# DeltaNet stage of a three-block forward pass: order of the VectorE and ScalarE work between weight tiles

## The reference

```python
decay = jnp.exp(jnp.where(lower_incl, gc[..., :, None] - gc[..., None, :], -jnp.inf))
kb = k * beta[..., None]
lmat = jnp.where(strict, jnp.einsum('bhnid,bhnjd->bhnij', kb, k) * decay, 0.0)
tinv = lax.linalg.triangular_solve(eye + lmat, ..., left_side=True, lower=True)
u = tinv @ (v * beta[..., None])
w = tinv @ (kb * jnp.exp(gc)[..., None])
attn = jnp.einsum('bhnid,bhnjd->bhnij', q, k) * decay
k_dec = k * jnp.exp(g_last[..., None] - gc)[..., None]
# scan over 4 chunks of 64 tokens with a 128 x 128 state for each of 8 heads
v_new = u_i - w_i @ state
o_i = q_i @ state + attn_i @ v_new
state = state * jnp.exp(gl_i) + k_i.T @ v_new
# then
o = rms_norm_2(o, norm_w) * jax.nn.silu(z)
g_nsa, g_dn = jnp.split(jax.nn.sigmoid(merge_g), 2, axis=-1)
mixed = g_nsa * (o_nsa @ w_up_nsa) + g_dn * (o_dn @ w_up_dn)
```

## Time and profile before

| | before |
|---|---|
| median of three runs | 2406.88 us |
| profiled execution, its time | 2404.23 us |
| profiled execution, its span | 2402.5 us |
| mean granted TensorE clock | 0.991 |
| VectorE busy | 1468.0 us (61%) |
| ScalarE busy | 1296.1 us (54%) |
| GpSimd busy | 18.3 us (1%) |
| HBM over the span | 169 GB/s |

### The profile page before, as it was taken

How to read it: one execution, slowest core, us unless ns; L and a number is a source line. 1 busy time by engine, 2 the same in 40 slices (tenths; PEclk the granted TensorE clock), 3 DMA queues, 4 the chain that set the end, 5 groups by cost and what they waited for, 6 DMA issues and landing times.

```text
span 2402.5 us, 33358 instructions
## 1 busy us (share of the span) xinstructions
PE 2337.5 (97%) x12514; PEld 1985.3 (83%) x12514; DVE 1468.0 (61%) x2567; ACT 1296.1 (54%) x2393; POOL 18.3 (1%) x38
## 2 busy tenths in 40 slices
PE   8999999899999899999999999999999999999998
PEld 7877788788888899778787887888888888888887
DVE  4554565675665655886676566656666666665554
ACT  5645455665565544775555545555555555554444
POOL 1000000000000000000000000000000000000000
PEclk9999999999999999999999999999999999999999
DMA  6555566456435465656453225655666666665554
GB/s 213 158 167 149 165 203 194 139 158 183 124 123 192 142 184 165 186 158 197 143 166 118 83 80 176 220 185 180 186 188 189 186 191 185 188 205 190 191 190 167
DMA packets 247404, 408.94 MB, mean 170 GB/s; under 512 B 29713, under 2 KB 62529, under 8 KB 246865
## 3 DMA queue, kind: packets, MB, share of 16 engines
q1 hardware_dynamic: 243392, 393.20, 54.7%
q0 software_dynamic: 3136, 10.26, 1.2%
q10 hardware_dynamic: 720, 3.42, 0.4%
HBM read 400.53 MB, written 6.29 MB: 169 GB/s over the span
## 4 chain that ended last, share of the span: by engine, by line
PE 89%; DVE 5%; ACT 4%; issue 1%; DMA 0%; SPq 0%; DVEq 0%; ACTq 0%
PE banks L361 50%; PE banks L335 14%; PE banks L355 9%; PE banks L337 7%; DVE weights_low L306 2%; PE banks L644 1%; ACT weights_high L303 1%; PE banks L804 1%; PE banks L2221 1%; PE banks L2210 1%; PE banks L1681 1%; PE banks L815 0%; DMA weight_ring<-in_w_gla_in 0%; PE banks L1102 0%; PE banks L2283 0%
## 5 line engine op out<-in xcount | busy, mean ns | idle before, releaser
L306 DVE TENSOR_TENSOR weights_low<-weight_ring,weights_high 128x512 fp32r<-128x512 f32 (+3 forms) x1512 | 1007.1, 675 | 841.7 <-ACT weights_high L303 812.5
L303 ACT CAST weights_high<-weight_ring 128x512 fp32r<-128x512 f32 (+3 forms) x1512 | 910.2, 609 | 1002.8 <-PE banks L361 637.8
L361 PE MATMUL banks<-weights_high,hidden_T 128*128 128x512 f32 x3008 | 865.9, 400 | 10.8 <-DVE weights_low L306 9.6
L361 PEld LDWEIGHTS banks<-weights_high,hidden_T 128*128 128x128 f32 x3008 | 557.0, 189 | 135.3 <-issue 12.8
L361 PE MATMUL banks<-weights_low,hidden_T 128*128 128x512 f32 x1504 | 466.7, 391 | 0.0
L335 PE MATMUL banks<-hidden_T,weights_high 128*128 128x512 f32 x1408 | 385.1, 394 | 0.6 <-DVE residual L2829 0.6
L361 PEld LDWEIGHTS banks<-weights_low,hidden_T 128*128 128x128 f32 x1504 | 283.3, 188 | 61.6
L335 PEld LDWEIGHTS banks<-hidden_T,weights_high 128*128 128x128 f32 x1408 | 240.4, 189 | 32.9 <-DVE residual L2829 0.8
L337 PEld LDWEIGHTS banks<-hidden_T,weights_low 128*128 128x128 f32 x1408 | 216.5, 189 | 30.3
L337 PE MATMUL banks<-hidden_T,weights_low 128*128 128x256 f32 x1408 | 224.4, 281 | 0.0
L355 PE MATMUL banks<-hidden_T,weights_high 128*128 128x256 f32 (+3 forms) x1120 | 185.3, 286 | 6.9 <-DVE weights_low L306 5.9
(11 more groups left out here) (400 smaller groups left out, 1737.2 us busy)
## 6 DMA issues: line engine op xcount, KB each, us to landing
weight_ring<-in_w_in SPq DMA_DIRECT2D x168, 512.0 KB, 3.6
weight_ring<-in_w_gla_in SPq DMA_DIRECT2D x96, 512.0 KB, 3.8
weight_ring<-in_w_gate SPq DMA_DIRECT2D x88, 512.0 KB, 3.7
weight_ring<-in_w_ffn_up SPq DMA_DIRECT2D x88, 512.0 KB, 3.6
weight_ring<-in_w_down SPq DMA_DIRECT2D x88, 512.0 KB, 3.8
weight_ring<-in_w_mla_in SPq DMA_DIRECT2D x49, 512.0 KB, 3.6
weight_ring<-in_w_gla_out SPq DMA_DIRECT2D x32, 512.0 KB, 4.2
weight_ring<-in_w_mla_out SPq DMA_DIRECT2D x32, 512.0 KB, 4.3
```

Source lines behind the costliest of these rows:

```text
L303: nc.scalar.copy(hi, raw).then_inc(high_ready, 1)
L306: nc.vector.tensor_tensor(lo, raw, hi.bitcast(F32), ALU.subtract).then_inc(low_ready, 1)
L361: last = pe.matmul(ps[:, b + t, 0:width], a[:, t * P:(t + 1) * P], w, start=(k == 0 and n_th == 0), stop=(k == kt - 1 and n_th == 2))
```

## The change

Four edits, all of them in the order and the place of work of ScalarE and VectorE; TensorE's queue is the same but for the name of one semaphore.

- VectorE does one filler step instead of three ahead of the decay work of a pass, and (2, 6) instead of (1, 3) after its halves. The first corner of the system is taken there, and `b_lt` stands for it too.
- The block with the turned keys leaves VectorE. ScalarE copies the turned keys from PSUM into `d_kd` as they are, ahead of its scaling of the values, and signals `b_keys` after both. TensorE's turn of the corner waits for `b_keys` instead of `b_ct`.
- VectorE makes `d_kg` from `d_kd` in SBUF after levels 1 and 2 (a half in each) and scales `d_kd` in place by the decay left after level 5. Its fillers in levels 0 and 1 are (1, 2) and 2 instead of 1 each.
- After the second pass ScalarE has its two filler steps between the squares instead of ahead of them and one more behind, and the splits of the first four tiles of the up product stand between the last turns on both engines, instead of behind them and the fillers.

```diff
                 for hf in HALVES:
-                    pe.wait_ge(b_ct, 2 * bt + hf + 1)
+                    pe.wait_ge(b_keys, 2 * bt + hf + 1)
...
                     act.wait_ge(b_tok, 2 * bt + hf + 1)
+                    Sc(act.copy(part_of(d_kd, hf), bank(hf, 0)))
                     for j, m in enumerate(ms(hf)):
...
+                    act.sem_inc(b_keys, 1)
                     fill(2)
...
-                fill(2)
-            squares(bt, 1)
+                if bt + 1 < DN_H // HB:
+                    fill(2)
+            squares(bt, 2)
+            fill(1)
             next(turns)
             next(turns)
+            prod_up.split(act, 0, 0, 0)
             roots(bt)
-            next(turns)
-            next(turns)
-            fill(3)
-            prod_up.prime(act)
-            fill(1)
+            for k in range(1, 3):
+                next(turns)
+                prod_up.split(act, 0, 0, k)
+            prod_up.split(act, 0, 0, 3)
+            fill(4)
...
             for bt in range(DN_H // HB):
-                fill(3)
+                fill(1)
...
                     V(v.tensor_tensor(lt, bank(hf, 0), lt, ALU.mult))
+                    corner(0, hf)
                     v.sem_inc(b_lt, 1)
-                    fill((1, 3)[hf])
-                for hf in HALVES:
-                    v.wait_ge(b_tok, 2 * bt + hf + 1)
-                    V(v.tensor_tensor(by_head(d_kg, hf), bank_heads(hf, 0), col(d_bg, bt, hf), ALU.mult))
-                    V(v.tensor_tensor(by_head(d_kd, hf), bank_heads(hf, 0), col(d_eleft, bt, hf), ALU.mult))
-                    corner(0, hf)
-                    v.sem_inc(b_ct, 1)
-                    fill(2)
+                    fill((2, 6)[hf])
...
                     v.sem_inc(b_xd, 1)
-                    fill(1)
+                    fill((1, 2)[hf])
...
-                    fill(1)
+                    fill(2 if lv == 1 else 1)
                     if lv <= 2:
                         decayed_queries(bt, (2 * lv - 2, 2 * lv - 1))
+                        if lv == 1:
+                            v.wait_ge(b_keys, 2 * bt + 2)
+                        hf = lv - 1
+                        V(v.tensor_tensor(by_head(d_kg, hf), by_head(d_kd, hf), col(d_bg, bt, hf), ALU.mult))
...
+                for hf in HALVES:
+                    V(v.tensor_tensor(by_head(d_kd, hf), by_head(d_kd, hf), col(d_eleft, bt, hf), ALU.mult))
                 for ch in range(NCH):
...
             inverses(bt)
-            next(turns)
-            next(turns)
+            prod_up.split(v, 0, 0, 0)
+            for k in range(1, 3):
+                next(turns)
+                prod_up.split(v, 0, 0, k)
+            prod_up.split(v, 0, 0, 3)
             fill(4)
-            prod_up.prime(v)
             v.wait_ge(b_nrs, bt + 1)
```

More of the change, by code:

```diff
@@ L2122, in program @@
             "row_inputs", "rows", "row_exps", "decay_ready", "products", "systems_ready", "tokens"))
-        (b_ct, b_t1, b_t1c, b_x, b_xd) = (sem("dn_inv_" + n) for n in ("corner", "corner_times", "corner_times_copied", "update", "updated"))
+        (b_keys, b_t1, b_t1c, b_x, b_xd) = (sem("dn_inv_" + n) for n in ("tokens_copied", "corner_times", "corner_times_copied", "update", "updated"))
         (b_uw, b_uwc, b_sc, b_vn, b_sn, b_si, b_in, b_ind) = (sem("dn_" + n) for n in (
```

## The result

| | before | after |
|---|---|---|
| median of the runs made beside each other | 2406.85 us (4 runs, 2406.26 to 2407.22) | 2389.61 us (4 runs, 2387.57 to 2390.39) |
| profiled execution, its time and span | 2404.23, 2402.5 us | 2388.96, 2387.2 us |
| mean granted TensorE clock | 0.991 | 0.993 |
| TensorE busy | 2337.5 us | 2332.0 us |

The ratio is 0.9928 (95% interval 0.9914 to 0.9942): 17.2 us faster by the medians, 15.3 by the two profiled executions. In the code after, VectorE's L2471 to L2475 have become L2476 to L2480, the corner L2443, L2490 and L2491 are L2489 and L2490, ScalarE's new copy is L2367, its scaling L2370; the sigmoid is L2719, VectorE's multiply behind it L2727, and GpSimd's store and loads are L3003 and L3013.

The account below looks back on a forecast made before the run. TensorE, busy 97%, bounds the kernel; only its waits or half-clock time can be won. Savings 6.2 + 6.0 + 2.1 = 14.3 us take the profiled 2404.23 to 2389.9, or 2392.6 against the median 2406.88; range 2388.8 to 2400.0.

Parts of the forecast that it names:

- What bounds the kernel: Whole kernel: TensorE is busy 97% of the span, so only its waits or half-clock time can be won.
- Decay work sooner and keys copied out: First and second DeltaNet pass: earlier VectorE decay work and ScalarE's key copies shorten TensorE's waits, saving 6.2 and 6.0 us.
- The waits forecast as 0.6 and 1.2: First pass, TensorE: some 0.6 us before tile 10 and 1.2 us before the second level-1 product.
- In the levels nothing is lost: Both passes: waits hide VectorE's moved multiplies, costing nothing; without cover, 2.9 us a pass.
- The tail: Up product: 4.0 us gained before tile 4, 2.0 lost waiting for the gates' path through DRAM; worth 2.1.
- A second fall of the clock: Rival, chance 0.26: a new 2.0 us wait near 1487 lowers TensorE's clock, costing 1.6 us; 2394.2 us.
- The gate path does not bind: Rival, chance 0.11: the gates' path through DRAM does not delay TensorE, so the tail gives 4.0 us; 2390.7 us.
- ScalarE has over 1.2 us to spare for each half: Rival, chance 0.12: ScalarE finishes the keys over 2.2 us late, corner turns wait, half of 12.2 is lost; 2398.7 us.
- The change does what it says: Rival, chance 0.05, said it doesn't: decay work still waits for exps or products, waits move a few tiles; 2405 us.
- Six splits in a row: Rival, chance 0.04: VectorE's splits 10 to 15 delay level 0 to 1303 in both passes, 5.5 us slower; 2412.4 us.
- The range: Whole kernel: 2388.8 (tail whole, 1.9 more waits gone) to 2400.0 us (half the levels lost, a clock fall).

Follow-up runs that it names:

- the extra multiplies: The changed kernel with the multiply that makes d_kg made three times in levels 1 and 2; 2393.74 us, ratio 0.9945.
- the kernel with the loads in another order: The changed kernel with GpSimd's gate loads issued in the order round 1, round 0, 2, 3; 2396.30 us, ratio 0.9958.
- levels alone: The changed kernel with its last part undone, so the tail is that of the kernel before; 2392.30 us, ratio 0.9942.
- decay sooner alone: The kernel before with only the order of VectorE's splits changed, one ahead of the decay work instead of three; 2397.10 us, ratio 0.9963.
- the decay late: The changed kernel with the decay work back behind three splits; 2398.70 us, ratio 0.9969.

## Why the prediction was right, and where it was off

The median lies 3.0 us under the forecast and inside the range, near its lower end.

- **What bounds the kernel**: right. Only TensorE's waits and its lower clock moved the time. VectorE's busy time fell by 0.3 us, ScalarE's rose by 2.2.
- **Decay work sooner and keys copied out** (6.2 and 6.0): measured 6.16 and 5.93. The start of tile 16 was forecast as 1303.3 and came at 1303.86 in an execution whose DeltaNet began 0.55 later; tile 44 at 1397.0 less 6.2 of the first pass is 1390.8, and it came at 1391.21. The waits forecast as 0.6 and 1.2 were 0.42 and 1.06. The experiments add what the sum could not: the first edit alone brings 5.3 and 4.2, and the second alone 1.6 and 1.6.
- **In the levels nothing is lost**: right, no wait stands there after. For level 2 of the second pass the text had a cover of 0.05 us left; the extra multiplies show 0.1, by far the tightest of the four places.
- **The tail** (2.1): the term that was mis-sized. It measured 3.6. The first part was right, 4.07 for 4.0. Taken back were 0.40 and 0.06, not 2.0. The step that failed is the length of the second gate load, taken over as 7.5 from the earlier trace rows; it measured 5.6. Measured from the DeltaNet's start and with the passes' 12.2 taken off, the store is issued 2.0 sooner (forecast 1.9), GpSimd's wait for it is 0.3 longer (6.35 against 6.03), and the load is 1.9 shorter. So the sigmoid begins 3.6 sooner where 1.9 was forecast. The mechanism was right for the new kernel: the sigmoid of after starts with the landing, and in the kernel with the loads in another order each microsecond of it is one of TensorE. In before itself the landing was not what decided, or not alone: the table load ended at 1486.04, last by less than 0.1 us. I took one load, issued 0.26 us behind a weight load, as the length in the new kernel. In after that neighbour was issued 2.27 us ahead; whether this is why the load was shorter stays open.
- **A number that agrees by luck.** Put on top of the levels, the tail's edit is worth 2.1 in the table (217.4 against 215.3), as forecast. But it is 2.5 gained before up tile 4 and 0.4 taken back, not 4.0 and 2.0, because in levels alone the clock had stayed up without it.
- Beside this: the Trainium skill, DMA: Bandwidth & Descriptors, section on the anatomy of a DMA on the gpsimd path, gives an estimate of 3.2 us for this load. The traces do not agree: the second gate load took 5.4 to 7.5 us. The 4.0 that this page would have left in the tail was nearer to the result than my 2.1, though its length was not.
- **The rest of the miss**: of 17.2 us, 15.8 lie in the stretch of the table, 1.5 more than the sum. The other 1.4 lie outside it, between profiled executions and medians, and say nothing of the mechanism. Before's profiled execution was 2.65 under its median, and the forecast added these 2.65 again; after's was 0.65 under its own, with its DeltaNet 0.55 later. Against the profiled execution the forecast was 2389.9, and 2388.96 came.
- **The rivals.** A second fall of the clock did not come, as the new wait was 0.22, not 2.0; with 2.97 it does. "The gate path does not bind" gave the nearer time (2390.7). Its conclusion was wrong, as the path binds in after, but its reasons were partly right, and I dismissed them too easily. The second gate load was shorter in the new kernel, and the table load had ended at 1486.04 in before. The landing at 1486.0, which I held against it, could not decide between the two. ScalarE has over 1.2 us to spare for each half. The change does what it says. Six splits in a row end at 1292.52 + 0.69, 2.7 us before the turned corner is there; split 15 was placed at 1292.5.
- **The range**: its upper end adds up to 2400.3 by its own terms (2392.6, 6.1 and 1.6), not 2400.0; this changes nothing.

## What to carry to other kernels

Where one engine's queue feeds TensorE both weight splits and the links of a dependent chain, what is needed later goes behind what is needed sooner: putting the chain's first operations two splits forward brought most of the passes' gain, with no work removed. A wait found behind the one that was taken away should be worked out in the time frame of the new kernel. A DMA in it is a range from several rows of the trace with different neighbours, not one row. And a difference of one or two microseconds in 2400 is read from the traces, between the same instructions, since the medians carry falls of the clock from stretches that were not touched.

## What the runs showed of the hardware

- **The same wait with and without a fall of the clock.** After a wait of 2.22 us ahead of up tile 0 the granted clock fell to 0.50 (1.2 GHz) in before and in decay sooner alone, and stayed at 1.00 (2.4 GHz) in levels alone, with the same tiles ahead of it. Waits of 1.34 and 1.73 us in a row were followed by the lower level in before, 0.55 and 1.73 in decay sooner alone were not. Waits of 2.62, 2.64 and 2.97 were. So a fall cannot be told from the length of the last wait alone; what else decides, these runs leave open. I had expected the limit to lie between 1.92 and 2.22.
- **Its price** was 1.6 us each time it could be taken alone: 18.09 against 19.66 to up tile 4, and 10.97 against 12.58 to up tile 20. In the first pass of before it was more: from the second level-1 product to tile 16 it took 5.14 us (1304.33 to 1309.47), in after 2.80.
- **Loads of the same 512 KB** on GpSimd's queue, the first of a row of four issued 0.5 us apart, took 3.9 to 5.9 us, the second 5.4 to 7.5, the fourth up to 9.6. With SyncE's weight load at nearly the same distance ahead (2.27 and 2.29 us) the second took 5.6 in after and 6.5 with the decay late. So the length of one such load in one trace is good to about 1 us at best.
